# Matmul operands moved by 64 bytes in the stages of 256 columns, and the gated ones in the stages of 512

## What is computed

```python
def swiglu(h, w_in, w_out):
    gate, up = jnp.split(h @ w_in, 2, axis=-1)          # 1024 -> 2 x 2816
    return (jax.nn.silu(gate) * up) @ w_out             # 2816 -> 1024
# first block, layers 0 and 1 (x and ctx, 256 tokens each)
x = x + 0.5 * gt1 * swiglu(modulate(x, ...), ffn1_wi[i], ffn1_wo[i])      # ctx alike
x = x + gt2 * (conformer_conv(hx, ...) if i == 0 else windowed_gqa_sink(hx, hc, ...))
x = x + 0.5 * gt3 * swiglu(modulate(x, ...), ffn2_wi[i], ffn2_wo[i])      # ctx alike, layer 0
# second block, layers 0 and 1 (x alone)
h = h + mixer(rms(h, norm_mix[i]))                      # layer 0: moba and dilated; layer 1: nsa
h = h + swiglu(rms(h, norm_ffn[i]), w_gate, w_up, w_down)
h = h + sigmoid(rms(h, norm_ple[i]) @ w_ple_gate[i]) * (p[i] @ w_ple_proj[i])
```

## Time and profile before

| | us |
|---|---|
| median of 3 runs | 2622.47 |
| lowest, highest | 2618.04, 2627.67 |
| profiled execution, first to last instruction | 2621.3 |
| PE busy in it | 2505.4 |
| PEld busy | 2139.4 |
| DVE busy | 1336.2 |
| ACT busy | 1155.1 |

### The profile page before, as it was taken

The page is one execution under the profiler, slowest core; times in us unless marked ns, Lnnn a source line. Parts: engine busy times, 40 slices in busy tenths (PEclk is TensorE's granted clock), DMA queues, the critical chain, the costliest instruction groups (busy, mean ns, idle before and its releaser), DMA issues.

```text
span 2621.3 us, 39926 instructions
## 1 busy us (share of the span) xinstructions
PE 2505.4 (96%) x15799; PEld 2139.4 (82%) x15799; DVE 1336.2 (51%) x2003; ACT 1155.1 (44%) x1827; POOL 23.7 (1%) x37
## 2 busy tenths in 40 slices
PE   6999999998999999999999998999889998979998
PEld 4777787875777778777788777999869998869998
DVE  4323334896523233422333466555777665776665
ACT  3323323464433322332322356554556555565554
POOL 0000000000000000000000000000100001000000
PEclk8999999999999999999999999999999998999999
DMA  7444542210344442244423221445424455403554
GB/s 312 167 161 170 186 172 88 89 49 1 114 181 170 161 159 96 104 185 160 170 102 112 82 96 65 176 176 193 166 79 177 180 194 196 157 34 116 189 188 150
DMA packets 52724, 374.88 MB, mean 143 GB/s; under 512 B 5822, under 2 KB 7034, under 8 KB 8736
## 3 DMA queue, kind: packets, MB, share of 16 engines
q1 hardware_dynamic: 50000, 358.63, 37.0%
q0 software_dynamic: 2208, 14.37, 1.6%
q10 hardware_dynamic: 432, 0.73, 0.1%
HBM read 372.55 MB, written 7.39 MB: 145 GB/s over the span
## 4 chain that ended last, share of the span: by engine, by line
PE 89%; DVE 6%; ACT 2%; issue 1%; DMA 1%; SPq 0%; ACTq 0%; DVEq 0%
PE acc L1855 27%; PE acc L1856 26%; PE acc L1857 26%; PE bank L1932 3%; DVE wlo L1308 1%; PE bank L1959 1%; DMA ada_raw<-in_slabs 1%; PE acc L2352 1%; DVE prod L598 1%; DVE sc L1757 1%; PE acc L2326 1%; PE bank L1990 1%; DVE prod L1674 0%; PE Mod L1942 0%; DVE hlo L1392 0%
## 5 line engine op out<-in xcount | busy, mean ns | idle before, releaser
L1308 DVE TENSOR_TENSOR wlo<-raw,whi 128x1024 fp32r<-128x1024 f32 x534 | 646.0, 1223 | 901.4 <-ACT whi L774 900.9
L774 ACT ACTIVATE whi<-raw 128x1024 fp32r<-128x1024 f32 x534 | 556.2, 1055 | 969.8 <-PE acc L1857 912.5
L1855 PE MATMUL acc<-hhi,whi 128*128 128x256 f32 (+1 forms) x2808 | 949.1, 338 | 30.0 <-DVE hlo L1392 13.2
L1856 PE MATMUL acc<-hlo,whi 128*128 128x256 f32 (+1 forms) x2808 | 935.2, 333 | 0.0
L1857 PE MATMUL acc<-hhi,wlo 128*128 128x256 f32 (+1 forms) x2808 | 934.9, 333 | 0.0
L1855 PEld LDWEIGHTS acc<-hhi,whi 128*128 128x128 f32 x2808 | 538.8, 192 | 115.0 <-issue 58.6
L1857 PEld LDWEIGHTS acc<-hhi,wlo 128*128 128x128 f32 x2808 | 538.7, 192 | 50.3
L1856 PEld LDWEIGHTS acc<-hlo,whi 128*128 128x128 f32 x2808 | 539.2, 192 | 49.7 <-issue 1.7
L1855 PE MATMUL acc<-ghi,whi 128*128 128x512 f32 (+1 forms) x1056 | 354.5, 336 | 0.0
L1856 PE MATMUL acc<-glo,whi 128*128 128x512 f32 (+1 forms) x1056 | 354.3, 336 | 0.0
L1857 PE MATMUL acc<-ghi,wlo 128*128 128x512 f32 (+1 forms) x1056 | 354.3, 336 | 0.0
(11 more groups left out here) (286 smaller groups left out, 2201.1 us busy)
## 6 DMA issues: line engine op xcount, KB each, us to landing
raw<-in_slabs SPq DMA_DIRECT2D x329, 1024.0 KB, 4.8
ada_raw<-in_slabs SPq DMA_DIRECT2D x10, 1024.0 KB, 26.1
skew_dram<-lines_dram POOLq DMA_DIRECT2D x1, 6144.0 KB, 23.7
bt<-skew_dram POOLq DMA_DIRECT2D x4, 1024.0 KB, 9.4
x<-in_x_in SPq DMA_DIRECT2D x1, 2048.0 KB, 17.8
mlp<-in_slabs POOLq DMA_DIRECT2D x2, 1024.0 KB, 6.1
out<-x SPq DMA_DIRECT2D x1, 1024.0 KB, 4.8
rope<-in_rope POOLq DMA_DIRECT2D x1, 512.0 KB, 4.0
```

The costliest lines, as they stand in the source:

```text
L774: nc.scalar.activation(whi[:, n % 2, cols], raw_of(n, cols), ACT.Copy).then_inc(ready, 1)
L1308: nc.vector.tensor_tensor(wlo[:, n % 2, cols], raw_of(n, cols), whi[:, n % 2, cols].bitcast(F32), ALU.subtract).then_inc(low, 1)
L1855: nc.tensor.matmul(out, w[0], xx[0], start=first, stop=False)
L1856: nc.tensor.matmul(out, w[0], xx[1], start=False, stop=False)
```

## The change

Four things are done.

- `hhi`, `hlo`, `ghi` and `glo` each become 32 float32 (128 bytes) longer and are allocated flat. What stands behind them moves up as the table above shows.
- `place_operands` gives every stage a home, an offset in `hhi` and `hlo`: 0 behind a norm of 512 columns, unless the stage after that norm is `qkv`; 16 float32 (64 bytes) behind every other norm, up to the next norm. `g_home`, the offset in `ghi` and `glo`, is 16 in stages of 512 columns and 0 in those of 256. ACT and DVE write and PE reads at these offsets; `phi` and `plo` follow their stage's home.
- The two small buffers `kcsq` and `kcr` of the `nsa` stage, 256 bytes each, are dropped and use a part of `arow`, which is free by then. This makes room.
- Names: the argument `operand` of `tiles_of` becomes `made_by`, and `tokens_of` is given its operand.

The instructions of each engine are the same ones in the same order as before, with the same waits; only line numbers and addresses differ. `ohi` and `olo` get no home and keep their remainder of 64.

```diff
+        self.home, self.g_home = (0, 0), 0
...
+ROOM, G_ROOM = 32, 32
+
+
+def place_operands(plan):
+
+
+    home = (0, 0)
+    for st in plan:
+        if st.kind == "norm":
+            home = (0, 0) if st.T == 2 * S and plan[plan.index(st) + 1].kind != "qkv" else (16, 16)
+        st.home = home
+        st.g_home = 16 if st.T == 2 * S else 0
...
-        hhi = sb("hhi", [P, DT, 2 * S], F32R)
-        hlo = sb("hlo", [P, DT, 2 * S], F32R)
+        hhi_all = sb("hhi", [P, DT * 2 * S + ROOM], F32R)
+        hlo_all = sb("hlo", [P, DT * 2 * S + ROOM], F32R)
...
-            ghi = sb("ghi", [P, HT, 2 * S], F32R, ffn)
-            glo = sb("glo", [P, HT, 2 * S], F32R, ffn)
+            ghi_all = sb("ghi", [P, HT * 2 * S + G_ROOM], F32R, ffn)
+            glo_all = sb("glo", [P, HT * 2 * S + G_ROOM], F32R, ffn)
...
-            kcsq = sb("kcsq", [P, 64], F32, at)
-            kcr = sb("kcr", [P, 64], F32, at)
...
+        kcsq, kcr = arow[:, 0, 0:64], arow[:, 0, 64:128]
...
-        phi, plo = hhi[:, 0:2, S:2 * S], hlo[:, 0:2, S:2 * S]
...
+        def operand(st):
+
+            return tuple(a[:, at:at + DT * 2 * S].rearrange("p (a t) -> p a t", t=2 * S)
+                         for a, at in zip((hhi_all, hlo_all), st.home))
+
+        def ple_operand(st):
+
+            return tuple(a[:, at + S:at + S + 4 * S].rearrange("p (a t) -> p a t", t=2 * S)[:, :, 0:S]
+                         for a, at in zip((hhi_all, hlo_all), st.home))
+
+        def gated_operand(st):
+
+            return tuple(a[:, st.g_home:st.g_home + HT * 2 * S].rearrange("p (a t) -> p a t", t=2 * S)
+                         for a in (ghi_all, glo_all))
...
-                tiles_of(n, m, (hhi, hlo), st.T, i, per, paced=st if c == 0 else None).then_inc(slab_used, 1)
+                tiles_of(n, m, operand(st), st.T, i, per, paced=st if c == 0 else None).then_inc(slab_used, 1)
```

More of the change, by code:

```diff
@@ L835, in up_late @@
                 n, m = st.n0, st.m0
+                ghi, glo = gated_operand(st)
                 with act.Fori(0, 11) as i:
@@ L876, in residual @@
                 ks = st.slabs // 4
+                hhi, hlo = operand(st.feeds or st)
                 def last_squares(m):
@@ L936, in norm @@
                     preload(ACT.Sqrt)
+                hhi, hlo = operand(st)
                 x_final(act, st)
@@ L1890, in tiles_of, with tokens_of @@
                 return ins
-            def tokens_of(n, m, count, cols=SLAB_N, i=0, per=0, behind_first=None):
+            def tokens_of(n, m, op, count, cols=SLAB_N, i=0, per=0, behind_first=None):
+                hhi, hlo = op
                 for tt in range(count):
@@ L2032, in up_late @@
                 set_free(m)
-                tiles_of(n, m, (hhi, hlo), S, paced=st, mid=st.norm).then_inc(slab_used, 1)
+                tiles_of(n, m, operand(st), S, paced=st, mid=st.norm).then_inc(slab_used, 1)
                 half_pair(st, 1, n + 1, m + 1, 0, 2)
@@ L2038, in up_late @@
                         set_free(m + 2 + c, i, 2)
-                        tiles_of(n + 2 + c, m + c, (hhi, hlo), S, i, 2).then_inc(slab_used, 1)
+                        tiles_of(n + 2 + c, m + c, operand(st), S, i, 2).then_inc(slab_used, 1)
             def up(st):
@@ L2075, in residual @@
                 ks = st.slabs // 4
-                operand = None
+                made_by = None
                 if st.kind == "down":
-                    op, operand = (ghi, glo), (g_lo, {0: st.g0, HT - 2: st.g0 + 1})
+                    op, made_by = gated_operand(st), (g_lo, {0: st.g0, HT - 2: st.g0 + 1})
                 elif st.kind == "wo":
                     made = 2 + 8 * st.att0
-                    op, operand = (ohi, olo), (o_lo, {0: made - 1, DT - 1: made})
+                    op, made_by = (ohi, olo), (o_lo, {0: made - 1, DT - 1: made})
                 else:
-                    op = (hhi, hlo)
+                    op = operand(st)
                 with pe.Fori(0, 2) as i:
@@ L2154, in qknorm @@
                         set_free(m + c, i, 2)
-                        tiles_of(n + c, m + c, (hhi, hlo), S, i, 2, paced=None if c else st).then_inc(slab_used, 1)
+                        tiles_of(n + c, m + c, operand(st), S, i, 2, paced=None if c else st).then_inc(slab_used, 1)
                     for c in range(2):
@@ L2170, in tiles @@
                     there(p)
-                    tiles_of(n + p, m + p, (hhi, hlo), S, paced=st if p == CK else None).then_inc(slab_used, 1)
+                    tiles_of(n + p, m + p, operand(st), S, paced=st if p == CK else None).then_inc(slab_used, 1)
                 def head_sums(p):
@@ L2396, in plegate @@
                     set_free(st.m0 + c)
-                    tiles_of(st.n0 + c, st.m0 + c, (hhi, hlo), S, paced=None if c else st).then_inc(slab_used, 1)
+                    tiles_of(st.n0 + c, st.m0 + c, operand(st), S, paced=None if c else st).then_inc(slab_used, 1)
                     if st.next_norm and c:
```

21 lines of the change are left out of this document (13 added, 8 removed).

## The result

| | before | after |
|---|---|---|
| median, us | 2622.64 (4 runs) | 2639.56 (4 runs) |
| lowest, highest | 2618.04, 2627.67 | 2636.41, 2640.37 |
| profiled span | 2621.3 | 2638.4 |

The change made the kernel slower: ratio 1.0063, 95% interval 1.0048 to 1.0079. The forecast of 2582 and its whole range, 2573 to 2606, are missed; the rival that ended on the other side, 2646, is the nearest.

A forecast was written before the change was run, and what follows sets the result against it. PE was taken to bound the kernel, on lines 1855 to 1857. Terms of 29.9 + 9.8 + 1.0 - 0.3 = 40.4 us off the profiled 2621.3 gave 2580.9, with 1.2 added 2582; range 2573 to 2606.

The forecast's parts named there:

- the rival that ended on the other side, 2646: 512-column matmuls over hhi/hlo go to the 233 price, nothing else gains: 24.6 us slower, chance 0.06.
- What bounds the kernel: PE is busy 96% of the span, nearly 80% of it on lines 1855 to 1857, and gets its slabs in time.
- the remainder to 128: Operand addresses against the weights' address: the remainder to 128 decides a matmul's pitch; forecast 2582, chance 0.74.
- Term 1: 256-column matmuls over hhi/hlo, moved to remainder 64, go from 120.0 to 113.35 ns: 29.9 us gained.
- the parity: Matmul pitches in 6.67 ns slots: equal remainders go with even numbers, 18 and 34, a distance of 64 with odd, 17 and 35.
- Term 2: 512-column matmuls over ghi/glo, moved to remainder 0, go from 0.2333 to 0.227 us each: 9.8 us gained.
- What the sum took as free: The rest of the kernel was put at nothing, including ACT and DVE writing hhi and hlo 64 bytes further.
- The slower rival: All 3792 512-column matmuls over hhi/hlo cost 6.5 ns more and nothing else gains: 24.6 us slower, chance 0.06.
- Term 3: Lines 1907 to 1909 and 2283 to 2285, where whi moves and hhi gives the weights: 1.0 us gained.
- The buffer as the cause: Which buffer an operand is in, not its remainder, sets the pitch, so the shift does nothing: 2622, chance 0.08.
- Slabs that come late: The three 256-column up stages gain nothing at the new pace, 21 us less gain: 2602, chance 0.04.

The follow-up runs named there:

- e1: The changed kernel with its four buffers longer by 256 bytes each instead of 128, homes as changed: 2608.76 us, ratio 0.9935 to the kernel before.
- e10: As e1, but homes of 192 bytes in the stages of 256 columns, the same kernel as e8: 2588.93 us, ratio 0.9859 to the kernel before.
- e7: As e1, but homes of 32 bytes, not 64, in the stages of 256 columns: 2606.39 us, ratio 0.9933 to the kernel before.
- e9: The kernel of e1 once more, on another occasion and a different chip: 2611.94 us.
- e3: Buffers as in e1, with another home for almost every stage, as a table of pitches: 2632.48 us in one execution.
- e8: As e1, but homes of 192 bytes, not 64, in the stages of 256 columns: 2590.21 us, ratio 0.9868 to the kernel before.
- e12: Homes of 192 bytes in the 256-column stages alone, ghi and glo as before the change: 2597.4 us, ratio 0.9895 to the kernel before.
- e5: The kernel before, homes 0, with only hlo made 128 bytes longer, so the weights and everything behind move: 2637.91 us in one execution.

## Why the prediction was wrong

**What bounds the kernel** was right: PE, on these three lines, with its slabs in time. Neither the profiles of before and after nor those of e1 and e10 show PE waiting for `wlo` in an up or down stage (the one wait on these lines, 3.6 us in e1 and e10, is at the start of the kernel); e10 fetches at 196 GB/s in an up stage with PE busy throughout.

**The step that failed is the remainder to 128.** The forecast took from the table of addresses that 0 or 64 was all that mattered. In the kernel before no two operands differ by 128, so its prices could not tell a period of 128 from one of 256. The argument that should have excluded 256, pitches of 17, 18, 34 and 35 whole slots of 6.67 ns, was built on four numbers. The runs have pitches of 117.8, 118.7 and 116.7, which are 17.67, 17.8 and 17.5 such slots. These are averages, and 17, 18 and 18 slots would make 17.67 too; the single distances from start to start settle it. In the up stage of e1 between 1985 and 2085 all are 116 to 120 ns, where a mixture would need 113 and 120; in that of e7 all are 116 or 117; and the 233 of the kernel before are 230 or 231 and 235 or 236 by turns. The starts don't keep to whole slots, and the parity proved nothing.

**Term 1** (29.9 us) came as 8.1. Most of it failed on the place. Before the change the cheap case stood 192 bytes off the weights; the home of 64 bytes puts `hhi` 64 off, which is the same only with a period of 128. Of the up stages at (64, 64), none of six (e1, e9) ran at 113.3; at (192, 192), eight of ten did (e3, e8, e10, e12). e12, with homes of 192 bytes, recovers 27 us, near the term as it was worked out.

**Term 2** (9.8 us) came as nothing, since `glo` was at 128. With that repaired it is 10.5 us (e1): the size was right, and equal distances are the cheap place for 512 columns.

**What the sum took as free** cost most: 16.3 us on 512 columns over `hhi`/`hlo`, 7.0 us on down with 256. The sum has no term for either. The rows that say so were in the table of the addresses, `hlo` and `glo` 128 bytes further than `hhi` and `ghi` are. The slower rival named this widening and the stages of 512 columns, and put 24.6 us on them with nothing gained elsewhere. It was given 6 in 100. The rise was 4.3 ns per matmul instead of 6.5, because (0, 128) is at 231.1 in the `up` stages and at 233.3 in `pw1` and `pw2`. That its 2646 comes within 7 us is in part luck: it had neither the 7.0 us on down nor the 8.1 us gained over `hhi`/`hlo` with 256.

**Term 3**, the exchanged roles, was right: 0.8 us in its two steady runs, against 1.0. Line 1949 after (least, median and greatest length in ns), where the trace of before has 283 as the median for the same matmuls:

```profile
L1949 PE MATMUL acc<-whi,hhi x64: 276/276/680, 1555.5 to 2319.6; 128*128 128x256 f32 x64
```

Here `whi` moves and `hhi` is the weights; only the weights were moved. The distance counts, on either side. `whi` stands 64 bytes before `hhi`, which is 192 past it in the remainder to 256, so this term came to the place of 192 by chance, while term 1 did not (against `hlo` it stands at 64). In e1, where both stand at 192, the run in `qkv` is at 117.8 again, the other of the two pitches seen there.

**The other rivals.** The buffer as the cause falls with e1, where 64 bytes take 512 columns over `ghi`/`glo` from 233 to 227, and with e5. Slabs that come late were not seen in these stages.

**The page that spoke against the change.** The Trainium skill, "TensorE: Matmul & The Clock Gate", section "Part 2: What happens when you issue a matmul", has two independent read ports, so that loading the next weights takes nothing from the running matmul; that place has no effect was the prediction's conclusion from it. The traces disagree with that conclusion: e5 moves the weights by 128 bytes and leaves the moving operand where it was, and the pitch of 512 columns goes from 227 to 232. Whether the ports are the cause, no run shows.

## What to carry to other kernels

When operands are to be moved by a few bytes, compare the remainders of all operands that run together, and to a period at least twice the one you believe in; a buffer that grows moves all that stands behind it. Change one distance at a time, and give each stage another one in a single kernel: a profile with a dozen stages is a table of a dozen distances. In this kernel's stream of fp32r matmuls that each load new weights, the best places found were the weights' own remainder to 256 for a moving operand of 512 columns, and 192 bytes past it for one of 256, where two up stages in ten still ran at 117.8. For another kernel this is a place to begin a sweep.

## What the hardware showed beyond that

- The pitch of a matmul depends on the distance of the moving operand from its weights, modulo 256 bytes: 226.7 to 234.3 ns for 512 columns, 113.3 to 120 for 256. It isn't the distance alone: (192, 192) with 256 columns and (0, 128) with 512 each have two pitches.
- At (192, 192), one and the same loop runs at 113.3 or 117.8 ns for a whole stage, and the choice differed between two executions of one program, e1 and e9, on two chips. A down stage differs by 2.3 us with it, an up stage by 4.6. Whether the spread between runs (e1: 2604.42 to 2613.64) comes from it isn't shown; the kernel before has one as wide (2618.04 to 2627.67).
- The state seems to be handed on: behind an up stage at 117.8 or 116.7, nine of ten down stages at (192, 192) ran at 117.8.
